# Fourier branch of a two-layer hybrid block: cosine and sine sums kept apart for half the positions

## The reference

```python
def fourier_mix(z):                       # z: (1, n, 384)
    u = z.astype(jnp.float32).reshape(bsz, n, FOURIER_GROUPS, FOURIER_GROUP_W)   # 6 groups of 64
    y = jnp.fft.fftn(u, axes=(1, 3), norm="ortho").real
    return y.reshape(bsz, n, W_FOURIER).astype(z.dtype)
```

## Time and profile before

| what | value |
|---|---|
| median of 3 runs | 2316.08 us (2312.39 to 2317.49) |
| the profiled execution | 2316.2 us, span 2314.4 us, mean granted clock 0.993 |
| TensorE busy | 2251.6 us, 97% |
| VectorE, ScalarE, GpSimd busy | 53%, 22%, 38% |
| Fourier position transform (L794) | 1% of the chain that ended last |
| tables dft_l and dft_c | 2048 KB and 512 KB, landing 8.1 and 8.2 us from issue |

### The profile page before, as it was taken

The page is one execution under the profiler, slowest core; times in us unless marked ns, Lnnn a source line. Parts: engine busy times, 40 slices in busy tenths (PEclk is TensorE's granted clock), DMA queues, the critical chain, the costliest instruction groups (busy, mean ns, idle before and its releaser), DMA issues.

```text
span 2314.4 us, 30244 instructions
## 1 busy us (share of the span) xinstructions
PE 2251.6 (97%) x12396; PEld 1785.3 (77%) x12396; DVE 1221.4 (53%) x1830; ACT 500.8 (22%) x785; POOL 871.1 (38%) x476
## 2 busy tenths in 40 slices
PE   5899999999999999999999999999999999999998
PEld 4688798865568878888888887868865687888886
DVE  5879921044656264445665525499435574552453
ACT  2232122045430131011110112221345402110111
POOL 2123133310014434343444443336520055866663
PEclk9999999999999999999999999999999999999999
DMA  7163252343244323333223232734520254322222
GB/s 278 48 155 94 96 151 105 112 149 105 84 172 165 129 78 118 120 110 110 82 79 104 89 130 101 206 109 141 179 77 24 80 176 146 109 97 95 100 92 72
DMA packets 104543, 270.05 MB, mean 117 GB/s; under 512 B 23008, under 2 KB 41824, under 8 KB 102624
## 3 DMA queue, kind: packets, MB, share of 16 engines
q1 hardware_dynamic: 67200, 183.53, 23.5%
q10 hardware_dynamic: 37216, 84.68, 11.1%
HBM read 230.28 MB, written 37.88 MB: 116 GB/s over the span
## 4 chain that ended last, share of the span: by engine, by line
PE 90%; DVE 5%; DMA 2%; ACT 1%; ACTq 1%; issue 0%; POOL 0%; DVEq 0%; POOLq 0%
PE ps L416 66%; PE ps L927 3%; PE ps L809 2%; PE ps L942 2%; PE ps L425 2%; PE ps L519 2%; PE ps L970 2%; PE ps L794 2%; DVE t_in L1892 1%; PE ps L431 1%; PE ps L743 1%; PE ps L817 1%; PE ps L837 1%; PE ps L870 1%; PE ps L824 1%; DMA zs_d<-zs 1%
## 5 line engine op out<-in xcount | busy, mean ns | idle before, releaser
L1145 POOL TENSOR_SCALAR whi<-raw 128x1024 fp32r<-128x1024 f32 x236 | 260.2, 1102 | 1391.5 <-PE ps L416 1091.8
L1148 POOL TENSOR_TENSOR wlo<-raw,whi 128x1024 fp32r<-128x1024 f32 x236 | 611.4, 2591 | 19.7
L416 PE MATMUL ps<-hh,whi 128*128 128x512 f32 (+1 forms) x1560 | 469.5, 357 | 0.3 <-DVE ada L545 0.3
L416 PE MATMUL ps<-hh,wlo 128*128 128x512 f32 (+1 forms) x1560 | 463.6, 354 | 0.0
L416 PE MATMUL ps<-hl,whi 128*128 128x512 f32 (+1 forms) x1560 | 463.2, 353 | 0.0
L416 PEld LDWEIGHTS ps<-hh,whi 128*128 128x128 f32 x1560 | 255.0, 188 | 48.8 <-issue 5.7
L416 PEld LDWEIGHTS ps<-hl,whi 128*128 128x128 f32 x1560 | 255.2, 188 | 44.5 <-issue 0.7
L416 PEld LDWEIGHTS ps<-hh,wlo 128*128 128x128 f32 x1560 | 254.4, 188 | 43.3
L1825 DVE SCALAR_TENSOR_TENSOR x<-ps,ada,x 128x512 f32<-128x512 f32 x120 | 75.5, 659 | 351.0 <-PE ps L416 350.9
L416 PE MATMUL ps<-midh,whi 128*128 128x512 f32 (+1 forms) x768 | 234.7, 360 | 1.5 <-DVE midl L1855 1.5
L416 PE MATMUL ps<-midl,whi 128*128 128x512 f32 (+1 forms) x768 | 231.8, 356 | 0.0
(11 more groups left out here) (215 smaller groups left out, 2862.6 us busy)
## 6 DMA issues: line engine op xcount, KB each, us to landing
raw<-in_w_main SPq DMA_DIRECT2D x236, 512.0 KB, 3.3
ada_mixer<-in_ada_w SPq DMA_DIRECT2D x32, 512.0 KB, 3.3
ada_gap<-in_ada_w SPq DMA_DIRECT2D x24, 512.0 KB, 8.5
ada_mlp<-in_ada_w SPq DMA_DIRECT2D x24, 512.0 KB, 3.7
g_d<-gt ACTq DMA_DIRECT2D x24, 384.0 KB, 2.3
gl<-g_d ACTq DMA_DIRECT2D x8, 1152.0 KB, 5.5
ada_first<-in_ada_w SPq DMA_DIRECT2D x16, 512.0 KB, 19.0
cout_d<-cz SPq DMA_DIRECT2D x12, 512.0 KB, 5.0
```

Of the source, the lines that this page charges most:

```text
L416: ins = pe.matmul(ps[:, p % 4, a:b], ww[:, w % W_SLOTS, kw * P:(kw + 1) * P], xx[:, kx, a:b], start=(first and i == 0 and j == 0), stop=(l ...
L1145: pool.tensor_scalar(whi[:, u, :], raw[:, u % 2, :], 1.0, 0.0, ALU.mult, ALU.add).then_inc(w_split.sem, 1)
L1148: pool.tensor_tensor(wlo[:, u, :], raw[:, u % 2, :], whi[:, u, :].bitcast(F32), ALU.subtract).then_inc(w_split.sem, 1)
```

## The change

Cosine and sine parts get PSUM regions of their own (columns 0 to 511 and 512 to 1023 of the pair), and only positions 0 to n/2 are computed, 257 and 129 columns. ScalarE copies the sine part into a new buffer `odd`; VectorE forms the first half as the difference and the second half, written backwards, as the sum (`fold`). In layer 0 the folds stand between scan steps 53 and 54, in layer 1 ahead of the query scale. The loads of `cout` go behind the copies. The tables have 257 and 129 columns.

```diff
+SCAN_FOLD = 54
+HL, HC = LAT // 2 + 1, CTX // 2 + 1
...
+        odd = at("odd", EXTRA + 9216, [P, 3, HL + HC])
...
-            for tab, a, e, b0, nb in ((dft_l, 0, LAT, 0, 4),) + ((dft_c, LAT, TOK, 4, 2),) * (n > LAT):
+            for tab, a, e, b0, nb in ((dft_l, 0, HL, 0, 4),) + ((dft_c, HL, HL + HC, 4, 2),) * (n > LAT):
                 for b in range(nb):
                     for i in range(3):
                         for cs in range(2):
-                            ins = pe.matmul(ps[:, (3, 1, 2)[i], a:e], pq[:, b0 + b, i, cs * P:cs * P + P],
-                                            tab[:, b, cs, :], start=(b == 0 and cs == 0),
-                                            stop=(b == nb - 1 and cs == 1))
+                            ins = pe.matmul(ps[:, (3, 1, 2)[i], 512 * cs + a:512 * cs + e],
+                                            pq[:, b0 + b, i, cs * P:cs * P + P], tab[:, b, cs, :],
+                                            start=(b == 0), stop=(b == nb - 1))
                         if b0 + b == n // P - 1:
                             ins.then_inc(fr_b.sem, fr_b.mark((l, i)))
-                    if b0 + b in (1, 3) and b0 + b < n // P - 1:
-                        ins.then_inc(fr_tab.sem, fr_tab.mark((l, b)))
...
-            act.wait_ge(sn_scale.sem, sn_scale.at((l, 0)))
...
-            act.wait_ge(fr_tab.sem, fr_tab.at((l, 1)))
-            load_outputs(0)
-            if n > LAT:
-                act.wait_ge(fr_tab.sem, fr_tab.at((l, 3)))
-                load_outputs(1)
             for i in range(3):
                 act.wait_ge(fr_b.sem, fr_b.at((l, i)))
-                act.copy(of[:, i, 0:n], ps[:, (3, 1, 2)[i], 0:n]).then_inc(fr_evac.sem, fr_evac.mark((l, i)))
-            for j in range(2 if n > LAT else 1, 3):
+                width = HL + HC if n > LAT else HL
+                act.copy(odd[:, i, 0:width], ps[:, (3, 1, 2)[i], 512:512 + width]).then_inc(
+                    fr_odd.sem, fr_odd.mark((l, i)))
+            act.wait_ge(sn_scale.sem, sn_scale.at((l, 0)))
+            for j in range(3):
                 load_outputs(j)
...
+            def fold(i):
+
+                dve.wait_ge(fr_odd.sem, fr_odd.at((l, i)))
+                even = ps[:, (3, 1, 2)[i], 0:512]
+                for a, m, h in ((0, LAT, 0), (LAT, CTX, HL))[:2 if n > LAT else 1]:
+                    dve.tensor_tensor(of[:, i, a:a + m // 2 + 1], even[:, h:h + m // 2 + 1], odd[:, i, h:h + m // 2 + 1],
+                                      ALU.subtract)
+                    ins = dve.tensor_tensor(of[:, i, a + m - 1:a + m // 2:-1], even[:, h + 1:h + m // 2],
+                                            odd[:, i, h + 1:h + m // 2], ALU.add)
+                ins.then_inc(fr_evac.sem, fr_evac.mark((l, i)))
+
+            if l:
+                for i in range(3):
+                    fold(i)
             scale(0, zq, rs_q, KQ, n)
-            steps(SCAN_SPLIT, SCAN_EARLY)
+            if l == 0:
+                steps(SCAN_SPLIT, SCAN_FOLD)
+                for i in range(3):
+                    fold(i)
+                steps(SCAN_FOLD, SCAN_EARLY)
+            else:
+                steps(SCAN_SPLIT, SCAN_EARLY)
             steps(SCAN_EARLY, NC)
```

More of the change, by code:

```diff
@@ L186, in build @@
         pq = rest("pq", 49152, [P, TOK // P, 3, 2 * P])
-        dft_l = rest("dft_l", 89088, [P, LAT // P, 2, LAT])
-        dft_c = rest("dft_c", 105472, [P, CTX // P, 2, CTX])
+        dft_l = rest("dft_l", 89088, [P, LAT // P, 2, HL])
+        dft_c = rest("dft_c", 105472, [P, CTX // P, 2, HC])
         c64 = rest("c64", 109568, [P, 2 * P])
@@ L339, in build @@
         fr_b = signal("fr_b")
-        fr_tab = signal("fr_tab")
+        fr_odd = signal("fr_odd")
         fr_evac = signal("fr_evac")
@@ L1470, in act_layer @@
                         hi, src = ((osh, osm), (ofh, of))[u // 3]
+                        if u == 3:
+                            act.wait_ge(fr_evac.sem, fr_evac.at((l, 2)))
                         act.copy(hi[:, u % 3, 0:n], src[:, u % 3, 0:n]).then_inc(os_hi.sem, os_hi.mark((l, u)))
@@ L2136, in dft @@
     def dft(n):
-        k = np.outer(np.arange(n), np.arange(n)) % n * (2 * np.pi / n)
+        k = np.outer(np.arange(n), np.arange(n if n == 64 else n // 2 + 1)) % n * (2 * np.pi / n)
         return np.cos(k), np.sin(k)
@@ L2141, in lay_out @@
         c, s = dft(n)
-        m = np.stack([c, -s], 1) / np.sqrt(n)
-        t[name] = f(m.reshape(n // P, P, 2, n).transpose(1, 0, 2, 3).astype(np.float32))
+        m = np.stack([c, s], 1) / np.sqrt(n)
+        t[name] = f(m.reshape(n // P, P, 2, n // 2 + 1).transpose(1, 0, 2, 3).astype(np.float32))
     c, s = dft(64)
```

## The result

The changed kernel takes 2329.74 us (median of 4, 2324.36 to 2335.63) against 2316.18: a ratio of 1.0068, 95% interval 1.0046 to 1.0089. It is **slower**, by 13.6 us where 3.1 were forecast, and above the forecast range. A second set of runs gave 1.0069 (1.0047 to 1.0090).

A forecast was written before the change was run, and what follows sets the result against it. TensorE, 97% busy, was taken to bound the kernel up to its next wait, the scan's chain ahead of the SSM outputs. Layer 0 -5.2, layer 1 +3.5, clock +4.8 gave +3.1 on 2316.2: 2319.3 us, range 2311.5 to 2325.0.

The forecast's parts named there:

- the chain of waits: Around the Fourier stage: SSM outputs need snat and toep behind VectorE's scan; slack 2.9 us in layer 1, 10.5 in layer 0.
- the clock: Behind both new TensorE waits at the SSM outputs: half granted clock, 2.4 us each, +4.8; bounds 0 and 2.9 each.
- TensorE's saving: Fourier matmuls of 257 and 129 columns instead of 512 and 256: 12.95 us in layer 0, 10.45 in layer 1.
- The folds: Additions on VectorE, 12 in layer 0 and 6 in layer 1: 4.3 and 2.55 us, hidden from the gate slots.
- The line: Fit through VectorE times of PSUM-input operations of 96, 256 and 512 columns: 0.425 us for 257, 0.29 for 129.
- slots 1 to 3: Gate slots needing the folds' banks: folds end 250.8 before 254.2 and 1548.95 before 1549.3, so no wait.
- Layer 0: TensorE reaches SSM outputs at 304.2, waits 7.6 us for toep until 311.9; gains 5.2 of its 12.95.
- Layer 1: 14 GpSimd pairs in the scan instead of 13; states at 1639.5 against 1636.0: loses 3.5 us, TensorE waits 13.9.
- The row at 142.43: Profile evidence for the clock's price: TensorE had idled 2.28 us, 96 records took 12.73 instead of 10.8, 1.9 lost.
- the upper case: Dear bounds: folds add 2.7 and 1.6 us, the clock 1.0; +8.4, 2324.6.
- Rival (a): Slower by more than 0.2% (4.6 us): folds before steps 54 and 44 push the scan; up to 2324.6; chance 0.32.
- Rival (c): Faster by nearly the whole 23.4 us, 2293, if SSM outputs do not wait for the scan; chance 0.08.

## Why the prediction was wrong

The direction was right and the chain of waits held. One term, the clock, was mis-sized by a factor of seven, and it carried the sum out of the range: forecast -5.2 + 3.5 + 4.8 = +3.1, measured -8.2 + 2.8 + 18.6 = +13.2.

- **TensorE's saving**: forecast 12.95 and 10.45 us, measured 12.6 (25.70 less 13.12, from the start of the stage to the first gate tile) and 10.2. Right.
- **The folds**: forecast 4.3 and 2.55, measured 3.2 and 2.0. The line put 0.425 us on a 257-wide operation. That is what one lasts (0.41 to 0.43), but the next one starts 0.335 behind it: the same slope, but a fixed part of 0.07 instead of 0.16. The line runs through the rows of 96 and 512 columns and 0.05 below that of 256, so "well held by three sizes" was too strong. Right in kind, a quarter too dear. The Trainium skill (VectorE: DVE Perf Modes, the TRN2 errata) gives a PSUM source 62 fixed cycles more than an SBUF source. The prediction's estimate from it, 1.2 us more for the 18 operations, which the sum left out, would have been further from what was measured. They hid from slots 1 to 3, as forecast; no wait appears there.
- **Layer 0**: forecast -5.2, measured -8.2. The forecast had GpSimd's sixth split start 2.2 us ahead of the scan's end, and so one more pair in the scan; here it started 0.05 us ahead and cost nothing. The folds' 1.1 us less are half of that. Most of the other half is TensorE's: its seven gate tiles took 8.48 us each here instead of the 8.32 of the earlier trace rows, so the splits came later. The kernel before shows both paces too (8.48 in the two profiles with only layer 1's outputs moved), and what sets them is not shown. In the five profiles of this form with 8.32 the folds are just as short, but the sixth split started 1.1 to 6.3 us before the scan's end, and the waits are 4.4 to 8.9. The mechanism, toep's load behind VectorE's copy behind the scan, was right; the wait hangs on an edge that one execution meets and another does not, and that the profiled one missed is luck.
- **Layer 1**: forecast +3.5 with a wait of 13.9; measured +2.8 with 13.0. Right.
- **The clock**: "I take 2.4 each, +4.8; bounds 0 and 2.9 each". Measured 1.9 in layer 0, and in layer 1 14.9 in the stage and 1.8 in the gate tiles behind it, **16.7**. This is the step that failed. The price was read from places where gate-like tiles of 512 and 256 columns followed the idling, and carried over to a stage of another kind. The row at 142.43, whose matmuls resemble layer 0's outputs, gave 1.9, and layer 0 cost 1.9. For layer 1's stage no row after idling existed, and I gave it the same bound of 2.9 rather than the honest one, twice the length of the stage: 16 us more. With that the upper case would have been 2324.6 - 2.9 + 16 = 2338, above the result. No rival held it.
- **Rival (a)** had the right side but the wrong mechanism: it put the excess on the folds, which were cheaper than taken. Rival (c) was wrong for this kernel; its number, 2293, was reached only with the outputs moved (2292).

## What to carry to other kernels

A wait on TensorE is priced by what runs behind it: here 2.5 us of waiting cost 18 us, and 13 us of useless matmuls in the place of a wait gained 11. So the upper bound of a new wait holds the stage behind it at half clock in full, unless a row shows that very stage recovering. Before work is taken off the bounding engine, the slack of each chain that runs beside it is read, and the added work of the change is charged to it. The room can then be made in the order of the work: later slots in layer 1 were worth nothing by themselves and turned +13.6 us into -18.3, and with one in layer 0 as well into -21.4.

## What the runs showed of the hardware

- The float32 output stage of layer 1 (64 columns behind a 128-column weight load) stayed at a granted clock of 0.50 for 27 to 31 us of unbroken work, behind waits of 13.0, 2.5, 2.4 and 1.8 us. It ran at 1.00 when TensorE came to it without a wait, or behind a wait of 0.5 us, or after 8.3 us of 512-column matmuls. Layer 0's stage of 96 columns was back at 1.00 within 4 to 7 us in all seven profiles, behind waits of 3.4 to 8.9 us. The width is the difference that one sees between the two stages, but no run changed the width alone, so that it is the cause is not shown.

Layer 0's stage in the changed kernel, by stretches of 2 us:

```profile
308.00:310.00 2.00, 2.00 (x15) 2.00 (x14) 1.44 (x2) 0.00 (x0) 0.07 (x1) 0.68 1.01 410
310.00:312.00 2.00, 2.00 (x12) 2.00 (x11) 0.00 (x0) 0.00 (x0) 0.00 (x0) 0.50 1.03 415
312.00:314.00 2.00, 2.00 (x19) 2.00 (x19) 0.00 (x0) 0.00 (x0) 0.00 (x0) 0.96 0.45 182
```

- VectorE operations that read PSUM and write backwards (255 and 127 columns) last as long as those that write forwards (257 and 129): 0.41 and 0.28 us. The odd width cost TensorE nothing: a record of 257 columns takes 10.7/48 = 0.22 us, like one of 256.
